# Three weight splits placed sooner, and the upper parts of one stage's activations taken by ScalarE

## The reference, cut to what matters

```python
def hybrid_layer(x, mem, g_mix, w_in, ...):
    h = rmsnorm(x, g_mix)
    z = h @ w_in
    qk_m, v_m, o_m, i_pre, f_pre, qkv_na, q_mem, gate_pre = jnp.split(z, split_idx, axis=-1)
    qk_m = jax.nn.silu(short_conv(qk_m, conv_w, conv_b))
    ...
    h_fwd = mlstm_chunkwise(q_m, k_m, vv, i_log[:, :, 0], f_log[:, :, 0])   # a gated recurrence over chunks
    h_bwd = flip(mlstm_chunkwise(flip(q_m), flip(k_m), flip(vv), ...))      # and the same backwards
    h_m = rmsnorm(h_fwd + h_bwd, ...) * jax.nn.sigmoid(o_m)
    q_na = rmsnorm(q_na, g_na_q) * (NA_HEAD_DIM ** -0.5)
    k_na = rmsnorm(k_na, g_na_k)
    h_na = neighbourhood_attention(q_na, k_na, v_na, rpb)
    h_mem = memory_cross_attention(q_mem, rmsnorm(mem, g_mem), w_mem_kv, g_mem_q, g_mem_k)
    gates = jax.nn.sigmoid(gate_pre).reshape(bsz, s, N_BRANCH, D_MODEL)
    y = (gates[:, :, 0] * (h_m @ w_proj_mlstm)
         + gates[:, :, 1] * (h_na @ w_proj_na)
         + gates[:, :, 2] * (h_mem @ w_proj_mem))
    x = x + y @ w_out
    u = rmsnorm(x, g_ffn) @ w_up
    return x + jnp.square(jax.nn.relu(u)) @ w_down
```

## Time and profile before

| | us |
|---|---|
| median of 3 runs | 3105.69 (3102.47 to 3107.93) |
| the profiled execution | 3104.95 |
| its span, first to last instruction | 3103.2 |
| TensorE matmuls busy | 2815.6 (91%) |
| VectorE busy | 1280.9 (41%) |
| ScalarE busy | 602.1 (19%) |
| GpSimd busy | 351.9 (11%) |

### The profile page before, as it was taken

The page is one execution under the profiler, slowest core; times in us unless marked ns, Lnnn a source line. Parts: engine busy times, 40 slices in busy tenths (PEclk is TensorE's granted clock), DMA queues, the critical chain, the costliest instruction groups (busy, mean ns, idle before and its releaser), DMA issues. The chain is left out here.

```text
span 3103.2 us, 42247 instructions
## 1 busy us (share of the span) xinstructions
PE 2815.6 (91%) x17384; PEld 2203.6 (71%) x17384; DVE 1280.9 (41%) x2157; ACT 602.1 (19%) x1455; POOL 351.9 (11%) x497
## 2 busy tenths in 40 slices
PE   7988888999999999999999998889999878888882
PEld 5866755888877888888887886777887745545541
DVE  6556487233354424243344653554434431111114
ACT  3244176010002001000002322331022201111111
POOL 1023200000001000000001002451011211111112
PEclk9988999999999999999999999999999979999996
DMA  4130120111121111111114320002112199999994
GB/s 145 42 89 17 55 91 22 41 55 51 48 105 41 54 41 41 54 42 67 41 45 110 47 45 1 2 2 55 44 28 106 64 362 418 415 414 408 402 378 185
DMA packets 131744, 362.92 MB, mean 117 GB/s; under 512 B 14808, under 2 KB 61016, under 8 KB 114144
## 3 DMA queue, kind: packets, MB, share of 16 engines
q1 hardware_dynamic: 120336, 341.70, 30.6%
q0 software_dynamic: 10512, 16.80, 1.5%
q10 hardware_dynamic: 704, 1.70, 0.1%
HBM read 349.21 MB, written 31.52 MB: 123 GB/s over the span
## 5 line engine op out<-in xcount | busy, mean ns | idle before, releaser
L495 PE MATMUL banks<-hT_upper,split_weights 128*128 128x512 f32 x2272 | 711.0, 392 | 9.0 <-DVE split_weights L138 4.4
L486 PE MATMUL banks<-split_weights,hT_upper 128*128 128x512 f32 x1536 | 484.7, 397 | 19.0 <-DVE hT_lower L138 8.3
L495 PEld LDWEIGHTS banks<-hT_upper,split_weights 128*128 128x128 f32 x2272 | 430.2, 189 | 99.6 <-issue 5.3
L495 PE MATMUL banks<-hT_lower,split_weights 128*128 128x512 f32 x1136 | 445.0, 392 | 0.0
L486 PEld LDWEIGHTS banks<-split_weights,hT_upper 128*128 128x128 f32 x1536 | 291.9, 191 | 81.9 <-issue 14.7
L486 PE MATMUL banks<-split_weights,uT_upper 128*128 128x512 f32 x1024 | 315.6, 389 | 0.0
L486 PE MATMUL banks<-split_weights,hT_lower 128*128 128x512 f32 x768 | 303.6, 395 | 0.0
L3102 PE MATMUL banks<-expert,ex_xT 128*64 128x256 f32 (+1 forms) x1632 | 262.1, 398 | 44.7 <-DMA expert<-in_w_up 20.3
L495 PEld LDWEIGHTS banks<-hT_lower,split_weights 128*128 128x128 f32 x1136 | 215.2, 189 | 44.6
L3102 PEld LDWEIGHTS banks<-expert,ex_xT 128*64 128x64 f32 (+1 forms) x1632 | 170.4, 149 | 101.0 <-issue 60.7
L486 PEld LDWEIGHTS banks<-split_weights,uT_upper 128*128 128x128 f32 x1024 | 191.9, 188 | 39.7
(11 more groups left out here) (489 smaller groups left out, 3711.0 us busy)
## 6 DMA issues: line engine op xcount, KB each, us to landing
expert<-in_w_gate SPq DMA_DIRECT2D x51, 1024.0 KB, 12.9
expert<-in_w_up SPq DMA_DIRECT2D x51, 1024.0 KB, 22.2
expert<-in_w_down SPq DMA_DIRECT2D x50, 1024.0 KB, 24.7
raw_weights<-in_w_in SPq DMA_DIRECT2D x38, 1024.0 KB, 6.3
raw_weights<-in_w_up SPq DMA_DIRECT2D x16, 1024.0 KB, 5.3
raw_weights<-in_w_down SPq DMA_DIRECT2D x16, 1024.0 KB, 5.0
hT<-in_w_gate SPq DMA_DIRECT2D x13, 1024.0 KB, 11.3
hT<-in_w_up SPq DMA_DIRECT2D x13, 1024.0 KB, 23.0
```

What stands on the lines that cost most here:

```text
L486: last = pe.matmul(bank, acts[x][:, r * KT // 2 + k, m * P:(m + 1) * P].bitcast(F32R), w[y][:, k, :].bitcast(F32R), start=(r == 0 and k == ...
L495: last = pe.matmul(out, w[x][:, k, c0:c0 + P].bitcast(F32R), acts[y][:, k, t0:t0 + nt].bitcast(F32R), start=(k == 0 and x == y), stop=(k = ...
```

## The change

The split of chunk 6 moves from behind the loop in `mlstm_inputs` to the head of its third round. In `attention_inputs` the splits of chunks 8 and 10 stand one unit sooner. In `project_norm`, where `whole` is given, ScalarE takes the upper parts of all tiles and VectorE, which waits for each of them, the lower parts only.

```diff
@@ mlstm_inputs, VectorE
             for m in range(TT):
                 dve.wait_ge(product, 18 + m + 1)
                 cols = slice(m * P, (m + 1) * P)
+                if m == 2:
+                    c.split_chunk(dve, C_NAQK)
                 nc.vector.tensor_tensor(whole[:, :, cols], hT[0][:, :, cols], hT[1][:, :, cols], ALU.add).then_inc(whole_back, 1)
                 dve.wait_ge(copied, 16 + m + 1)
                 nc.vector.tensor_tensor(og[:, m, :], og[:, m, :], c.k["g_mlstm"][:, :], ALU.mult)
-            c.split_chunk(dve, C_NAQK)
@@ attention_inputs
-    NEXT_SPLIT = {6: C_NAV, 8: C_NAV + 1, 14: C_MEMKV, 16: C_MEMKV + 1}
+    NEXT_SPLIT = {5: C_NAV, 8: C_NAV + 1, 13: C_MEMKV, 16: C_MEMKV + 1}
@@ project_norm
+        acts_upper = c.sem(mem, name + "_acts_upper")
@@ project_norm, ScalarE
+            if whole is not None:
+                for m in range(TT):
+                    cols = slice(m * P, (m + 1) * P)
+                    nc.scalar.activation(acts[0][:, :, cols].bitcast(F32R), whole[:, :, cols], ACT.Copy).then_inc(acts_upper, 1)
@@ project_norm, VectorE
                 for m in range(TT):
                     cols = slice(m * P, (m + 1) * P)
-                    split(dve, nc.vector, V, whole[:, :, cols], acts[0][:, :, cols], acts[1][:, :, cols]).then_inc(acts_split, 1)
+                    dve.wait_ge(acts_upper, m + 1)
+                    take_lower(nc.vector, acts[1][:, :, cols], whole[:, :, cols], acts[0][:, :, cols]).then_inc(acts_split, 1)
```

## The result

| | before | changed |
|---|---|---|
| median of 5 runs each | 3105.69 us | 3088.15 us (3087.66 to 3091.63) |
| ratio, 95% interval | | 0.9947 [0.9936, 0.9958] |
| span of the profiled execution | 3103.2 us | 3085.9 us |
| mean granted clock of TensorE | 0.955 | 0.961 |

In two later sets of runs, on chips 6 and 8 and each beside new runs of the kernel before, the same kernel gave 0.9957 and 0.9956, that is 13 us and inside the range.

The account below looks back on a forecast made before the run. TensorE, busy 91% of the span, was taken as the bound, so only its waits counted. 6.7 + 1.1 + 1.7 - 0.35 = 9.2 us less than 3104.95 gave 3095.8, with 0.74 for the median 3096.5; range 3091 to 3102.5.

Parts of the forecast that it names:

- What would show it: Signs: last tile 177.7, `mlstm` 178.7, ScalarE's table load 182.9; new 1 to 2 us transpose waits; others near 2.4 us.
- edit B: `attention_inputs`, chunk 8's split one unit sooner: minus 1.1 us, since transposes wait for scaled rows; not the full 4.7.
- edit C: `attention_inputs`, chunk 10's split one unit sooner: minus 1.7 us, VectorE's chain then setting TensorE's restart behind chunk 11.
- edit D: `project_norm`, ScalarE takes upper parts: plus 0.35 us, only tile 0 exposed; bounds 0 and plus 0.8.
- Edit A: `mlstm_inputs` to `mlstm`, chunk 6's split moved earlier: minus 6.7 us, block 3.9 sooner, first row landing sooner too.
- the spread of the runs: Range's lower end: 1 us allowed below the first rival's time, giving 3091.
- Rival 1: TensorE's clock stays up at border A or border C: 2.5 and 1.5 us more, 3092.5 with both; chance 0.22.
- border C: `attention_inputs`, TensorE's pause before its restart behind chunk 11, forecast to shrink from 2.71 to 2.4 us.
- border A: Border of `mlstm_inputs` and `mlstm`; TensorE's pause at 194.39 forecast to shrink from 4.39 to about 1.7 us.
- Rivals 2, 3 and 4: Only `mlstm`'s barrier moves: 3099.3, chance 0.13; that border gives nothing: 3103.2, 0.08; slow clock around units 8-11: 3111, 0.03.

Follow-up runs that it names:

- `a_only`: Only the move of chunk 6's split ahead of tile 2, against the kernel before: 3096.81 us, ratio 0.9975.
- `d_only`: Only ScalarE taking the upper parts in `project_norm`, against the kernel before: 3104.21 us, ratio 1.0001.
- the chunk 7 runs: Chunk 7's DMA issued behind `mlstm`'s first four rows in the kernel before: 3100.19 us; just ahead of the rows, with chunk 6's split moved: 3100.99 us.

## Why the prediction was wrong, step by step

- **The direction and the waits held.** Each sign that "What would show it" names is there: the last tile at 177.3 to 178.0, the block at 178.2, ScalarE at 183.3, the waits of 0.83, 1.65, 1.24 and 1.25 us in edit B, 2.37 us in edit C with VectorE's chain behind it, 2.46 us in edit D.
- **Edit A, forecast 6.7.** Start of `mlstm` and its length average 182.7 and 80.6 us over six profiles without edit A and 178.7 and 77.4 over the nine with it: 7.3 us, 4.1 at the barrier (forecast 3.9) and 3.2 behind it (2.8). In the changed kernel's own profile 7.65. The size is right, but by two errors: the landing took 5.1 us and not 4.2, and the stage then ran shorter by 1.4 us more than ScalarE's earlier start explains (3.24 less 1.86). The prediction also had ScalarE wait for VectorE's columns. Its table load doesn't: in `a_only` it starts at 181.77, ahead of the copy at 182.12.
- **Edit B, forecast 1.1.** From the transposes of the third run to the second pass it is 38.75 us before (297.93 to 336.68) and 37.66 after (290.35 to 328.01): 1.1. The transposes' order took back what the wait had lost, as worked out.
- **Edit C, forecast 1.7: the step of the mechanism that failed.** The waits gave 1.6 us (336.68 to 380.87 is 44.2 us, 328.01 to 370.63 is 42.6). The prediction let TensorE restart at the lower clock as behind 2.71 us, and had the 1.5 us of the upper clock only as a rival. The second pass fell from 7.0 to 5.6 us here, and the clock stayed up in all six profiles with edit C as it is. A pause of 2.4 us stood between two rows, 1.11 us with the clock kept and 2.71 with it lost; I took the answer of the nearer one, and it was wrong: at this place every pause up to 2.39 us kept the clock and every one from 2.45 us lost it. So edit C is worth 3.0 us.
- **Edit D, forecast plus 0.35.** Plus 0.36 at the first tile, and `d_only` the same time as before. The Trainium skill, "VectorE: DVE Perf Modes", section "Mode 2×_2P — use both read ports for one tensor", speaks against the edit, and the 0.36 us are near the 0.4 estimated from it (VectorE's cast takes 0.69 us, ScalarE's copy 0.96).
- **The sum.** With the sizes of its own profile, 7.65 + 1.1 + 3.0 - 0.36 is 11.4 us, so 3094.3. That is inside the range, so edit C's missing 1.3 us and edit A's 0.95 did not by themselves put the time below it. The other 6 us of the measured 17.5 lie outside the edits' stages or in the part of D's stage that D doesn't cause, and the kernel before moves by 2.7 of them without any edit.
- **The range: the term that was sized wrong.** What put the time below it is the 1 us that the range took "for the spread of the runs", with nothing for a stage's own scatter: two stages of the unedited kernel moved by 1.3 and 1.4 us together (its whole span by 2.1), and the experts by up to 4.3 us between kernels that leave them alone. Beside later runs of before the change gave 13 us twice, which the range would have held, so that the size of the first miss is in part luck. Of those 13, the averages of edit A (7.3) and the terms of B, C and D make 11.0; the last 2 us are not accounted for.
- **Rivals.** Rival 1 was right at border C and is open at border A. TensorE was granted 1.2 GHz in `mlstm` for 23.9 us in the kernel before and for 17.1 in the changed one, by the same windows of 1 us, which could be part of the 1.4 us above; but the second profile of the kernel before had 18.6 (stage 80.4 for 81.2). Rivals 2, 3 and 4 are refuted: by the chunk 7 runs, by `a_only`, and by a clock of 1.00 through edit B's four waits (no pair of matmuls behind them over 0.74 us).

## What to carry to other kernels

The split that sat last before the barrier cost twice here: its own 3.5 us, and 1.8 to 3.6 us of the next stage's first transfer, which stood behind the DMA that the split released. Look for both. When an edit shortens a pause of TensorE, find the longest pause in your profiles behind which the clock stayed up and the shortest behind which it fell. If the new pause lies between them, put the clock's price into the sum with its own chance, not only beside it. Before trusting a gain in a stage that wasn't edited, profile the unedited kernel twice.

## What was not expected of the hardware

- Behind the pause ahead of the last second pass of `attention_inputs`, TensorE kept 2.4 GHz at 2.36 to 2.39 us (six profiles) and fell to 1.2 GHz at 2.45 us (one) and at 2.53 us and more (eight). Where it falls right at the restart (1.22 us for the first pair) or two pairs later (0.73, then 1.06 us) the loss is nearly the same: 7.0 and 7.2 us for a pass of 5.6.
- The stretch at 1.2 GHz behind the pause at the start of `project_norm` differs from profile to profile of one kernel, 6.8 or 3.4 us. The stage takes 1.4 us less behind the shorter one, and the first unit of `gated_branches` 1.3 us less in the same profiles.
- The same 256 KB transfer with nothing shown ahead of it landed in 3.3 or in 4.7 to 5.1 us.
